# Expert outputs combined in turned form, and expert weights read four rows to a partition: a 32-expert decoder layer on one core

## The reference, cut to what matters

```python
x = x + einsum('btc,cd->btd', merged, w_out)
x = x + moe(rmsnorm(x, g_ffn), ...)          # top 4 of 32 experts, D_MODEL = D_FF = 1024
#   per expert e: gate = min(xb @ w_gate[e] + b_gate[e], 7); up = clip(xb @ w_up[e] + b_up[e], -7, 7)
#                 y = ((up + 1) * gate * sigmoid(1.702 * gate)) @ w_down[e] + b_down[e]
#                 x[token] += weight[token, e] * y
gate_p = sigmoid(rmsnorm(x, g_ple) @ w_ple_gate)
x = x + gate_p * (p @ w_ple_proj)            # per-layer embedding
y = rmsnorm(x, g_final)
```

## Time and profile before

| | us |
|---|---|
| median of 3 runs | 1276.72 (1275.2 to 1278.67) |
| the profiled execution, its own time | 1274.7 |
| its span, first to last instruction | 1273.0 |
| PE busy | 1242.8 (98% of the span) |
| DVE busy / ACT busy | 340.0 / 172.5 |
| read from HBM | 454.41 MB |

### The profile page before, as it was taken

One profiled execution on the slowest core, in us unless ns is written; L12 is line 12 of the kernel. 1 busy time (PEld: TensorE's weight loads), 2 busy tenths in 40 slices (PEclk: granted clock), 3 DMA queues, 4 the chain that ended last, 5 costly groups with the idle time before them and its releaser, 6 DMA issues.

```text
span 1273.0 us, 15848 instructions
## 1 busy us (share of the span) xinstructions
PE 1242.8 (98%) x6326; PEld 614.1 (48%) x6326; DVE 340.0 (27%) x685; ACT 172.5 (14%) x434; POOL 48.6 (4%) x129
## 2 busy tenths in 40 slices
PE   9999999999999999999999999999999999999996
PEld 7857888855434344343434433333334343434343
DVE  3155445423131213122121303122121212121224
ACT  3136204011101010000001000000000010101013
POOL 2221000200000000000000000000000000000001
PEclk9999999999999999999999999999999999999999
DMA  9947713698999999999999999999999999999961
GB/s 347 287 143 261 273 67 97 238 354 355 417 409 415 422 421 422 420 422 421 422 422 422 422 422 422 422 422 422 422 421 422 422 422 422 422 422 420 421 241 36
DMA packets 79782, 460.98 MB, mean 362 GB/s; under 512 B 8158, under 2 KB 9235, under 8 KB 30842
## 3 DMA queue, kind: packets, MB, share of 16 engines
q1 hardware_dynamic: 74512, 445.18, 85.5%
q0 software_dynamic: 3280, 10.75, 2.7%
q10 hardware_dynamic: 1946, 4.43, 1.0%
HBM read 454.41 MB, written 6.39 MB: 362 GB/s over the span
## 4 chain that ended last, share of the span: by engine, by line
PE 78%; DMA 15%; SPq 5%; DVE 1%; issue 1%; ACT 0%; POOLq 0%; POOL 0%; DVEq 0%
PE bank L1142 29%; DMA arena<-in_w_gate_dram 10%; PE bank L1172 9%; PE bank L704 9%; PE bank L1224 5%; SPq L445 5%; PE bank L746 4%; PE bank L1048 3%; PE bank L685 2%; DMA arena<-in_w_down_dram 2%; DMA arena<-in_w_up_dram 2%; PE bank L1158 2%; PE bank L1058 2%; PE bank L1281 1%; PE bank L1299 1%; PE bank L896 1%
## 5 line engine op out<-in xcount | busy, mean ns | idle before, releaser
L1142 PE MATMUL bank<-arena 128*64 128x512 f32 x2352 | 520.3, 595 | 14.1 <-DMA arena<-in_w_up_dram 7.9
L1142 PEld LDWEIGHTS bank<-arena 128*64 128x64 f32 x2352 | 166.3, 137 | 349.3 <-issue 347.8
L1172 PE MATMUL bank<-arena 128*64 128x512 f32 x720 | 159.1, 595 | 1.0 <-DMA arena<-in_w_gate_dram 1.0
L2061 DVE TENSOR_TENSOR arena<-bank,arena 128x512 f32<-128x512 f32 (+1 forms) x92 | 59.0, 683 | 244.9 <-PE bank L1224 244.6
L704 PE MATMUL bank<-arena 128*128 128x264 f32 x512 | 115.9, 388 | 0.0
L704 PEld LDWEIGHTS bank<-arena 128*128 128x128 f32 x512 | 96.8, 190 | 16.6 <-issue 0.2
L1172 PEld LDWEIGHTS bank<-arena 128*64 128x64 f32 x720 | 51.1, 137 | 107.1 <-issue 107.1
L1048 PEld LDWEIGHTS bank<-arena 128*128 128x128 f32 x512 | 62.8, 196 | 25.4 <-issue 25.2
L1224 PE MATMUL bank<-arena 128*128 128x512 f32 (+1 forms) x192 | 75.0, 602 | 0.0
L2043 DVE TENSOR_SCALAR arena<-bank 128x512 f32<-128x512 f32 x32 | 20.6, 686 | 193.3 <-PE bank L1142 193.3
L2054 DVE COPY arena<-bank 128x512 f32<-128x512 f32 x16 | 11.1, 692 | 223.2 <-PE bank L1142 223.2
(11 more groups left out here) (264 smaller groups left out, 762.9 us busy)
## 6 DMA issues: line engine op xcount, KB each, us to landing
arena<-in_w_gate_dram SPq DMA_DIRECT2D x128, 1024.0 KB, 25.8
arena<-in_w_up_dram SPq DMA_DIRECT2D x128, 1024.0 KB, 26.0
arena<-in_w_down_dram SPq DMA_DIRECT2D x126, 1024.0 KB, 26.1
arena<-in_w_in_dram SPq DMA_DIRECT2D x14, 2048.0 KB, 11.0
out_dram<-arena POOLq DMA_DIRECT2D x9, 512.0 KB, 6.9
arena<-in_state_hgrn_dram POOLq DMA_DIRECT2D x8, 512.0 KB, 8.1
arena<-sample_values ACTq DMA_DIRECT2D x8, 512.0 KB, 8.9
arena<-in_w_out_dram SPq DMA_DIRECT2D x4, 1024.0 KB, 8.0
```

The costliest lines, as they stand in the source:

```text
L1142: ins = pe.matmul(out[c][hp(one), :], src[:, k * P + CAP * one:k * P + CAP * one + CAP], w[one][:, j, halves(c)], start=(first and k == 0) ...
L1172: ins = pe.matmul(GATE[c][hp(one), :], xT_e[:, k * P + CAP * one:k * P + CAP * one + CAP], w[one][:, j, halves(c)], start=False, stop=False)
L2061: ins = dve.tensor_tensor(xs, src, xs, ALU.add)
```

## The change

**The combination is turned.** `y_sb` becomes the stationary operand, in eight slices of 128 columns, and `comb` the moving one: eight matmuls of 264 columns that give x transposed (128 features x 264 tokens). DVE adds each slice to `xt`, which holds x turned from the first pair on; `s_mixed` counts the slices. In the first pair PE adds the old `x` by matmuls with the identity (`turn_x1`), and in the second pair the down bias in turned form (`down_bias`), each in the same accumulation as the combination.

**The end.** DVE makes the turned x times `g_ple` straight from the last combination; PE turns `xt` back to rows (`turn_back`, 24 transposes) for the last additions and sums of squares. The embedding product of the samples moves from the last pair to the last but one.

**Weights of pairs 3 to 15** (index 2 to 14) are loaded as 2 MB "twins": 512 rows, four to a partition, 16 KB in one piece, in a ring of eight double places. PE waits at every second step g for both experts' twins. `h2` and `act_sb` are read with every fourth column for these pairs, and `gffn_4` is the gain in the matching order (four more small transposes early on).

```diff
+        twin = [view(HG + (g - 4) * 2 * GRAN if 4 <= g < 6 else R + (g if g < 4 else g - 2) * 2 * GRAN, 2 * GRAN).rearrange(
+            "p (j n) -> p j n", j=4) for g in range(RING // 2)]
...
+            parts_4 = [w.rearrange("o e (g p j) n -> (o e) g p j n", j=4, p=P) for w in (w_gate, w_up, w_down)]
...
+            def load_twins(i, e, count):
+
+                for at_ in range(count):
+                    sp.wait_ge(s_used, 2 * NGRAN * i + 2 * at_ + 4)
+                    sp.dma_start(twin[at_ % (RING // 2)], parts_4[at_ // 4 % 3][e + 2 * (at_ // 12) + at_ % 2, at_ // 2 % 2])\
+                      .then_inc(s_twin[at_ % (RING // 2)], 16)
...
-                load_experts(PER * q, 2 * PER * q)
-            load_experts(PAIRS - PER, NE - 2 * PER, split=True)
+                load_twins(PER * q, 2 * PER * q, NGRAN * PER)
+            load_twins(PAIRS - PER, NE - 2 * PER, NGRAN)
+            load_experts(PAIRS - PER, NE - 2 * PER, range(2 * NGRAN, 2 * NGRAN * PER - 2))
...
+            def down_bias(k):
+
+                rows = slice(k // 4 * NE, (k // 4 + 1) * NE)
+                pe.matmul(bank[2 + k % 4][:, 0:T], bias_dd[rows, (k % 4) * P:(k % 4 + 1) * P], wT[rows, :], start=True,
+                          stop=False, skip_group_check=True, tile_position=(rows.start, 0))
+
+            def turn_x1(k):
+
+                for t in range(NT):
+                    pe.matmul(bank[2 + k % 4][:, toks(t)], x[lanes(t), t, k * P:(k + 1) * P], ident[lanes(t), lanes(t)],
+                              start=(t == 0), stop=False, skip_group_check=True)
...
-                        ins = pe.matmul(XG[k // 4][:, (k % 4) * P:(k % 4 + 1) * P], h2[:, t, every_other(k)], oh[:, t, :],
+                        ins = pe.matmul(XG[k // 4][:, (k % 4) * P:(k % 4 + 1) * P], h2[:, t, every_other(k, j)], oh[:, t, :],
...
+                        if twins:
+                            at_ = NGRAN * n + 4 * m + g // 2 * 2 + one
+                            pe.wait_ge(s_twin[at_ % (RING // 2)], i0 * (16 * 2 * NGRAN // RING) - 48 + 16 * (at_ // (RING // 2) + 1))
+                            yield twin[at_ % (RING // 2)][:, 2 * (g % 2):2 * (g % 2) + 2]
...
-                def mix(t):
-
-                    for c in range(2):
-                        ins = mix_half(t, c)
-                    ins.then_inc(s_mix, 1)
...
+                def mix(ks, banks):
+
+                    for k in ks:
+                        out = bank[banks[k]][:, 0:T]
+                        if opening:
+                            turn_x1(k)
+                        if second:
+                            down_bias(k)
+                        pe.matmul(out, y_sb[:, k * P:(k + 1) * P], comb, start=not (opening or second), stop=True,
+                                  skip_group_check=True).then_inc(s_mix, 1)
...
+                        dve.scalar_tensor_tensor(xT[:, k, :], src, gple[:, k:k + 1], xT[:, k, :], ALU.mult, ALU.add)\
+                           .then_inc(s_xTk, 1)
+                        dve.tensor_tensor(xt[:, k, :], src, xt[:, k, :], ALU.add).then_inc(s_mixed, 1)
```

More of the change, by code:

```diff
@@ L173, in build @@
         gffn = view(take(KD), KD)
+        gffn_4 = view(take(KD), KD)
         power = view(take(1), 1)
@@ L410, in place_of @@
             return (at_ + (3 if at_ < 7 else 2)) % RING if at_ <= 16 else at_ % RING
+        first_loads = [sum(place_of(a) == g for a in range(2 * NGRAN * PER) if a not in early) for g in range(RING)]
+        last_loads = [sum(a % RING == g for a in range(2 * NGRAN, 2 * NGRAN * PER)) for g in range(RING)]
         block = ctx.enter_context(nc.Block())
@@ L1189, in pair @@
                 if not (opening or alone):
-                    pe.wait_ge(s_free23, i + 1)
+                    pe.wait_ge(s_mixed, 8 * (i + 1))
                     biases(range(2, 4), i + 1)
                 products(1, UP, xT_e, False).then_inc(s_up, 1)
-                pe.wait_ge(s_free6, i + 1)
-                if last:
-                    project("", 2, 0)
-                else:
+                if project_tiles:
+                    wait_drained(pe, ("pp", 2, 3))
+                if not last:
                     if second:
@@ L1200, in pair @@
                     pe.wait_ge(s_oh, i + 2)
-                    gather(range(4), s_used)
-                    gather_samples((0,))
+                    gather(range(4), s_used, n_used, next_apart)
+                    gather_samples((0,), next_apart)
                 pe.wait_ge(s_actr, i + 1)
-                pe.wait_ge(s_free45, i + 1)
+                pe.wait_ge(s_mixed, 8 * (i + 1))
                 if project_tiles:
                     wait_drained(pe, ("pp", 1, 1))
-                if second:
-                    wait_drained(pe, ("bd2", 1))
                 for c in range(2):
-                    turn_half(AT, act_sb, c, s_used if last else None).then_inc(s_aT, 1)
+                    turn_half(AT, act_sb, c, s_used if last else None, rows_apart).then_inc(s_aT, 1)
                 pe.wait_ge(s_ohw, i + 1)
@@ L1535, in rows_in, with projected, times_gain, pair @@
                     ins = act.activation(xT_e[:, k * P:(k + 1) * P], bank[6 + c][:, (k % 4) * P:(k % 4 + 1) * P], ACT.Copy,
-                                         scale=gffn[:, k:k + 1])
+                                         scale=gain[:, k:k + 1])
                 ins.then_inc(s_xe, 1)
-            def projected(r, t, n):
-                name = ("pp" + r, t, n)
+            def projected(t, n):
+                name = ("pp", t, n)
                 copy_out(name, pps[t][lanes(t), cols(t, n)], piece(name))
-            def pair(i, first=False, second=False, last=False, project_tiles=False):
+            def times_gain(pairs, done):
+                act.wait_ge(s_mixed, 8 * (pairs + 1))
+                for k in range(KD):
+                    act.activation(xT[:, k, :], xt[:, k, :], ACT.Copy, scale=gple[:, k:k + 1]).then_inc(done, 1)
+            def pair(i, first=False, second=False, last=False, project_tiles=False, next_gain=gffn):
                 if first:
@@ L1645, in _ @@
                         pair(b * PAIRS + e)
-                for t in range(NT):
-                    for n in pieces(t):
-                        projected("2", t, n)
                 finish("2")
```

342 lines of the change are left out of this document (133 added, 209 removed).

## The result

The changed kernel takes 1382.05 us (median; profiled execution 1382.71 us, span 1381.0), the kernel before 1276.43: a ratio of 1.0819, 95% interval 1.0795 to 1.0843. One of its four runs took 4524 us, which no other run of any kernel here did; the ratio is taken from the other three. The forecast of 1274.8 us with a range of 1267 to 1338 was wrong: 107 us too low, and 44 us beyond its slow end. Rival 1 named the place, the loads of the strided operand, but not the fall of the clock behind them, and so not the size.

A forecast was written before the change was run, and what follows sets the result against it. DMA was taken to set the pace from about 345 us to 1114.64, PE from there on. Terms summing to -1.9 us on the profiled 1274.7, with the median 2.0 above its profiled run, gave 1274.8 us; range 1267 to 1338.

The forecast's parts named there:

- Rival 1: Gather and turning: weight loads at every fourth column make PE the bound throughout; about +60, 1336 us; chance 0.33.
- What bounds the kernel: Kernel before: DMA sets the pace from about 345 us to 1114.64, PE from there to the end.
- slack of 3.3 us a pair: DMA-bound pairs: PE needs 56.3 us, DMA 59.6, so PE savings there buy nothing, up to 3.3 us per pair.
- a case in which the loads cost nothing: Whole kernel: the forecast's own case, 1274.8 us, bounds 1268 to 1283; chance 0.39.
- The signs of rival 1: GB/s line ragged and lower, waits for DMA vanish, the gather's 16 instructions take 3.9 to 4.0 us.
- First and second pair: Added turned work brings PE into the third pair about 5.5 us later; idle DMA costs +3.7 us, bounds +1 to +6.
- Larger packets: Weight loads ahead of the last wait: 16 KB packets for 8 KB save 1.3%, -9.6 us (-8.5 to -12.7).
- Coarser waits: Last wait for DMA, before a gate product's third quarter: PE waits two granules longer, +5.0 us, paid once.
- Combination, embedding product and end: Last two combinations before the final pair -1.9 us, moved samples' embedding product +1.0, end -0.5, four early transposes +0.4.

The follow-up runs named there:

- e7: e2 without the turning of the old x in the first pair and the down bias in the second: 1276.26 us, ratio 0.9988.
- e4: The changed kernel with a second, reordered copy of the token rows, so that the gather reads adjoining columns; 16 KB pieces kept: 1280.95 us, ratio 1.0030.
- e2: The kernel before with the turned combination alone; weights in 1 MB loads, two rows to a partition: 1288.35 us, ratio 1.0081.
- e9: e2 without the turning of the old x alone; the down bias in turned form stays: 1277.04 us, ratio 1.0013.
- e1: The changed kernel with two rows to a partition (8 KB pieces) for four, 2 MB loads and coarse waits kept: 1292.67 us, ratio 1.0107.
- e5: The kernel before plus four rows to a partition and a second, reordered copy of the token rows for the gather: 1276.66 us, ratio 0.9991.
- e6: The changed kernel with the gather's matmuls in twos between those of the down product: 1447.37 us, ratio 1.1326.

## Why the prediction was wrong, point by point

- **What bounds the kernel.** Right for before (though the line of the earlier trace rows has 25 slices at 420 to 422, not 27): e7 saves 0.9 us of PE in every pair and ends where before does. The slack of 3.3 us a pair, 4.2 with the cheaper combination, was the right gauge for rival 1.
- **The step that failed** is that the forecast's sum has no term for the loads of the strided operand. The edit to the gather's columns alone (e4) is worth 101 of the 107 us that were missing. The term stood in rival 1, and its weighing went wrong: its price of 0.118 us an instruction was right (0.115 measured, 0.233 for 0.118), but it got a chance of 0.33, behind the 0.39 of a case in which the loads cost nothing. What held it back were the loads' records of the earlier trace rows: 140 ns at one, 208 at two columns' distance for the turning, "which contradicts" the rule of two hits a line. But these records are longer than the steps from one instruction to the next: they overlap other work, and their mean is no cost. From start to start the turnings take 0.109 and 0.120 us, and plain matmuls 0.111 from adjoining columns (L787 of the earlier trace rows) and 0.118 in the gather: two columns' distance is nearly free, as the rule says. A unit of two floats would have doubled the gather already, so the trace of before spoke against it, and nothing in it spoke against the unit of four.
- **Rival 1's size.** 56 instructions a pair were counted, and 48 pay: the eight of the turning step at 0.120 us as before (L1075). So 5.5 us a pair for 6.6. On the other side neither the forecast nor rival 1 had a term for the clock, about 50 us: the larger mistake in rival 1's 1336. A pair takes 64.85 us where rival 1's own numbers give 56.3 - 0.9 + 6.6 = 62.0. From e4's side, a pair of its PE alone takes 55.1 and 48 instructions pay 0.121 (0.233 for 0.112), 60.9 together, so the clock is 3.9 us a pair.
- **The signs of rival 1** came as listed: GB/s ragged, waits for DMA gone, the gather 4.00 us.
- **First and second pair, +3.7 (bounds 1 to 6):** about 12 us (e2 less e7), 10.1 of it seen as idle DMA; e9 gives the place. `turn_x1` takes 7.6 us beyond the 3.8 of a plain combination, for 5.4; a slice of the down bias is 1.28 us for 0.92, because full and 32-row operands that take turns step at 0.32 us an instruction, not 0.23. These are sizes. The mechanism was right, but I followed only one hole in the queue, and there were two, with half clock in the second.
- **Larger packets, -9.6:** the DMA-bound pair steps 59.65 us with 8 KB pieces (in loads of 1 MB, and in those of 2 MB of e1) and 58.7 with 16 KB pieces, 0.039 us a MB for 0.032 taken, 1.6% for 1.3, within the bounds; e4 is 11.7 us under e1, of which some is a fall of the clock near 440 us that e1's profile has and e4's has not. What the sum left out is that a faster stream gains nothing while the ring is full (e5).
- **Coarser waits, +5.0:** 5 us at the last wait by the traces of e1 and e2, as said. But the sum took the wait as the only cost, and a full ring of double places costs another 4.8 at 420 to 450 us in e1. That the medians of e1 and e2 differ by just 4.3 is luck, within the spread of e2.
- **Combination, embedding product and end, -1.9 + 1.0 - 0.5 + 0.4:** together -1.0, against -0.5 by the medians of e7, which the noise covers; a combination takes 3.76 us from start to start for the 3.7 said.

## What to carry to other kernels

Before a layout is changed for the DMA's sake, count the 16-byte groups that TensorE's stationary operand then touches: 64 for 128 columns of float32 were nearly free here, beyond that the load grew with them. That was measured behind matmuls that step at 0.112 us; whether a load of 0.233 us would hide behind matmuls of 264 columns (0.235 us an instruction, L1242) was not tried. Take the cost of an overlapped load from the step between instructions, never from the mean of its record. A block of TensorE work that is bound by loads can have a second price behind it, the clock. Larger transfers pay only where the transfers set the pace; where the ring is full, or a last wait ends a phase, the small ones are better, so mix both.

## What was not expected of the hardware

- The clock fell to 1.2 GHz although PE hardly waited for anything (0.3 us in the weight products): 135 us of half clock in the span, 8.4 before. 26 of its 30 stretches, 116 us in all, begin in or behind a block of 24 slow gather instructions, some 6 us long; e4, with the same blocks at 0.112 us an instruction, has none there. The clock also falls once in the down bias's combination (e1, e2, 10.2 us), where no load is strided. The Trainium skill, "TensorE: Matmul & The Clock Gate", section "HAM oscillation — how this bites in real kernels", tells of it for waits for DMA; here it comes without such waits.
- Transposes pay nothing for four columns' distance (0.120 us an instruction, L1075), while matmuls from the same kind of operand double. Why is open; no run here tells.
- Instructions that alternate between shapes cost more than in blocks: 0.3 us a round of two changes in e6, 0.32 for 0.23 us an instruction in the down bias.
